# A transformer step's state-space mixer: its tiles re-ordered, conditioning loads in 1 MB steps, outputs of four tiles together

## The reference, cut to what matters

```python
ada = silu(c) @ ada_w + ada_b                      # 1024 x 6144: sh_m, sc_m, gt_m, sh_f, sc_f, gt_f
h = rms_norm(x, mix_pre_g) * (1 + sc_m) + sh_m
u, q, k, v, g_s, g_a = split(h @ w_in)             # u: 512 wide
bu = einsum('gpc,bsgc->bsgp', b_bar, u)            # 32 groups x 64 states, complex
state[t] = lam_bar * state[t-1] + bu[t]            # along 256 tokens
y = gelu(einsum('gcp,bsgp->bsgc', c_mat, state).real + d * u)
y = y * sigmoid(y @ w_glu)
q, k = rope(q), rope(k); y_a = attention(q, k, v)
merged = sigmoid(g_s) * (y @ w_s) + sigmoid(g_a) * (y_a @ w_a)
```

## Time and profile before

| | us |
|---|---|
| median of 3 runs | 2422.41 (2419.97 to 2429.88) |
| the profiled execution, its own time | 2422.49 |
| its span on the core | 2420.4 |
| PE busy | 2221.8 (92% of the span) |
| DVE busy | 960.2 (40%) |
| ACT busy | 605.2 (25%) |
| POOL busy | 27.4 (1%) |
| DMA, mean | 262 GB/s |

### The profile page before, as it was taken

One profiled execution on the slowest core, in us unless ns is written; L12 is line 12 of the kernel. 1 busy time (PEld: TensorE's weight loads), 2 busy tenths in 40 slices (PEclk: granted clock), 3 DMA queues, 4 the chain that ended last, 5 costly groups with the idle time before them and its releaser, 6 DMA issues.

```text
span 2420.4 us, 26402 instructions
## 1 busy us (share of the span) xinstructions
PE 2221.8 (92%) x10794; PEld 1292.1 (53%) x10794; DVE 960.2 (40%) x1683; ACT 605.2 (25%) x991; POOL 27.4 (1%) x44
## 2 busy tenths in 40 slices
PE   5888987999999899989975999989999999999998
PEld 3336842333333333333321888556887887555887
DVE  6782132222222222221213555344555554363655
ACT  2103020110101001001101443344434443154443
POOL 0010000000000000000000000000000000100000
PEclk9999989999999999999987999989999999999999
DMA  7534239999999999999997344224543453412541
GB/s 312 205 143 187 109 119 428 427 423 428 428 427 422 427 428 420 427 428 427 420 428 333 149 164 184 111 88 157 209 165 160 196 208 113 157 66 105 194 171 79
DMA packets 40765, 633.64 MB, mean 262 GB/s; under 512 B 4800, under 2 KB 4800, under 8 KB 5728
## 3 DMA queue, kind: packets, MB, share of 16 engines
q1 hardware_dynamic: 40640, 631.90, 63.4%
HBM read 630.84 MB, written 1.05 MB: 261 GB/s over the span
## 4 chain that ended last, share of the span: by engine, by line
PE 68%; DMA 18%; DVE 3%; ACT 2%; issue 1%; SPq 0%; ACTq 0%; DVEq 0%
DMA piece<-in_moe 18%; PE bank L1768 10%; PE bank L1684 10%; PE bank L1686 9%; PE bank L1685 9%; PE bank L599 6%; PE bank L1803 5%; PE bank L1218 3%; PE bank L1181 2%; PE bank L1749 2%; PE bank L1827 2%; PE bank L1013 1%; PE bank L1185 1%; PE bank L2088 1%; PE bank L1022 1%
## 5 line engine op out<-in xcount | busy, mean ns | idle before, releaser
L1768 PE MATMUL bank<-piece,xeT 128*64 128x512 f32 (+1 forms) x2304 | 453.1, 630 | 73.9 <-DMA piece<-in_moe 70.9
L1690 DVE TENSOR_TENSOR ffn_lo<-slot,ffn_hi 128x2048 fp32r<-128x2048 f32 x132 | 302.1, 2292 | 170.7 <-ACT ffn_hi L2213 165.1
L1768 PEld LDWEIGHTS bank<-piece,xeT 128*64 128x64 f32 (+1 forms) x2304 | 136.3, 133 | 357.9 <-issue 331.7
L1684 PE MATMUL bank<-ffn_hi,hT_hi 128*128 128x512 f32 x704 | 280.6, 399 | 8.4 <-DVE hT_lo L523 6.0
L2213 ACT ACTIVATE ffn_hi<-slot 128x2048 fp32r<-128x2048 f32 x132 | 251.7, 1913 | 130.2 <-PE bank L1686 115.2
L1686 PE MATMUL bank<-ffn_hi,hT_lo 128*128 128x512 f32 x704 | 275.5, 391 | 0.0
L1685 PE MATMUL bank<-ffn_lo,hT_hi 128*128 128x512 f32 x704 | 274.8, 390 | 0.0
L1875 DVE TENSOR_TENSOR hT<-hT,bank 128x512 f32<-128x512 f32 x144 | 92.2, 683 | 271.1 <-PE bank L1827 264.8
L599 PE MATMUL bank<-slot,hT 128*128 128x512 f32 (+1 forms) x384 | 169.2, 590 | 0.0
L1922 DVE TENSOR_SCALAR work<-bank 128x256 f32<-128x256 f32 x60 | 25.5, 425 | 355.2 <-PE bank L1775 355.2
L1684 PEld LDWEIGHTS bank<-ffn_hi,hT_hi 128*128 128x128 f32 x704 | 132.7, 189 | 38.1 <-issue 8.5
(11 more groups left out here) (610 smaller groups left out, 2336.9 us busy)
## 6 DMA issues: line engine op xcount, KB each, us to landing
piece<-in_moe SPq DMA_DIRECT2D x192, 2048.0 KB, 25.4
slot<-in_ffn SPq DMA_DIRECT2D x44, 3072.0 KB, 10.4
slot<-in_ada SPq DMA_DIRECT2D x6, 3072.0 KB, 10.0
slot<-in_merge SPq DMA_DIRECT2D x4, 3072.0 KB, 13.7
slot<-in_nsa_in SPq DMA_DIRECT2D x5, 2048.0 KB, 7.5
slot<-in_w_in SPq DMA_DIRECT2D x4, 2048.0 KB, 9.0
slot<-in_ada SPq DMA_DIRECT2D x3, 2560.0 KB, 9.0
slot<-in_hy_in SPq DMA_DIRECT2D x3, 2048.0 KB, 7.7
```

What stands on the lines that cost most here:

```text
L1684: pe.matmul(out, left[0], right[0], start=start, stop=False)
L1690: return dve.tensor_tensor(lo, x, hi.bitcast(F32), ALU.subtract)
L1768: pe.matmul(bank[n * c:n * (c + 1), :], x[:, kt, :], w[i][:, at:at + 512], start=kt == 0, stop=False)
```

## The change

1. **Outputs of four tiles together.** `outputs(q)` does the 16 matmuls of four tiles in one portion, the four tiles' matmuls interleaved, so that neighbours write to different 32-partition strips of the bank. It stands after the projections of tiles 4, 8, 12 and after the last tile. R gets six buffers: two in `ssm_r`, two each in the unused last 1 MB of ring slots 1 and 2; DVE waits for outputs only from tile 6 on, and for whole groups.
2. **Conditioning in 1 MB steps.** The six portions become 16 steps of four matmuls, one per tile, each on a load of its own of 1 MB in one of three thirds of slot 0; the bias and gain rows come as loads of 0.5 MB ("tails"). A step's load waits for the step three before it.
3. **Projection weights in halves.** q, k, v weights come as six loads of 1 MB in two halves of slot 2; PE does three projection matmuls per tile from tile 0 on, and none ahead of tile 0. At each half's end a drain of PE signals `qkv_half`.
4. **Angles earlier.** Sets 0 and 1 are made before `ada_vector(0)`, set 2 before the u copy, set 3 after tile 2; tile 0 needs three sets (`trig_done` 6).
5. **Rotary turn.** POOL's half goes to DVE. Both halves stand at the stage's end, behind the last skip, `ada_vector(2)` and the last v read.
6. `ada_vector(2)` moves from before tile 13 to behind the last skip, so the last four broadcasts wait for it.
7. The names of six semaphores are merged into two (`rows_dve`, `rows_pool`), with the counts that belong to that; nothing else in the other blocks changes.

```diff
+    def part(name, src, lo, width, slot, sub, done):
+        count[slot, sub] += 16
+        plan[name] = Part(src, lo, width, slot, 2048 * sub, held[slot, sub], sems[slot, sub], count[slot, sub])
+        order.append(plan[name])
+        held[slot, sub] = done
...
+    def qkv(h):
+        part(f"qkv{h}", ("w_in", 1 + h // 2), 2048 * (h % 2), 2048, 2, h % 2, (sig["qkv_half"], h + 1))
...
+        part(f"step{i}", ("ada", 3 * (g + 1) + n), ADA_GROUP * ADA_PARTS[n].index(kt), ADA_GROUP, 0, (i + g) % 3, (sig["ada_ready"], 3 + i + 1))
...
+    for what in ("q0 q1 s0 s1 s2 s3 s4 s5 q2 s6 s7 t1 q3 s8 s9 q4 s10 s11 s12 s13 q5 s14 s15 t2").split():
+        {"q": qkv, "s": ada_step, "t": ada_tail}[what[0]](int(what[1:]))
```

```diff
@@ ssm_vector
-        if j == 0:
-            dve.wait_ge(s["trig_done"], 8)
+        if jj == 0:
+            dve.wait_ge(s["trig_done"], 6 if q == 0 else 8)
...
-        if j >= 2:
-            dve.wait_ge(s["ssm_y_ready"], j - 1)
-        R = k["ssm_r"][:, j % 2, :, :, :]
+        if j >= SSM_ROWS:
+            dve.wait_ge(s["ssm_y_ready"], (j - SSM_ROWS) // SSM_Q + 1)
+        R = ssm_rows(k, j)
@@ ssm_tensor
-        pe.wait_ge(s["rotated"], j + 1)
...
+        pe.wait_ge(s["rotated"], SSM_Q * (q + 1))
         for n_, (c, trig, part) in enumerate(((0, 0, 0), (1, 1, 1), (2, 0, 1), (2, 1, 0))):
-            mm = pe.matmul(out, k["c_mix"][:, c, 32 * j:32 * j + 32], R[:, trig, part, :], start=n_ == 0, stop=n_ == 3)
+            for jj in range(SSM_Q):
+                j = SSM_Q * q + jj
+                mm = pe.matmul(k["ps"][6 + q % 2][32 * jj:32 * jj + 32, 0:S], k["c_mix"][:, c, 32 * j:32 * j + 32], ssm_rows(k, j)[:, trig, part, :], start=n_ == 0, stop=n_ == 3)
...
+        if at % KT == KT - 1:
+            pe.drain().then_inc(s["qkv_half"], 1)
...
+        for m in range(3 * j, 3 * j + 3):
+            project(m)
+        if j >= SSM_Q and j % SSM_Q == 0:
+            outputs(j // SSM_Q - 1)
+        if 10 <= j < 14:
+            ada_wide_tensor(k, pe, j - 10)
+        ada_step_tensor(k, pe, j)
+    outputs(SSM_TILES // SSM_Q - 1)
@@ the block of DVE
+            ssm_angles(f, dve, 1)
             ada_vector(f, dve, 0)
...
+            ssm_vector(f, dve, range(0, 3))
             ssm_angles(f, dve, 3)
+            ssm_vector(f, dve, range(3, 6))
             project_read(f, dve, 1, 2, qkv_dst, (0,), (2, 3))
+            ssm_vector(f, dve, range(6, 9))
             ada_vector(f, dve, 1)
+            ssm_vector(f, dve, range(9, 11))
             project_read(f, dve, 1, 2, qkv_dst, (1,), (2, 3))
+            ssm_vector(f, dve, range(11, 16))
+            ssm_skip(f, dve, 3)
             ada_vector(f, dve, 2)
             project_read(f, dve, 1, 2, qkv_dst, (2,), (2, 3))
+            for t in range(TT):
+                dve.wait_ge(*((s["proj_act"], 3) if t == 0 else (s["proj_dve"], 3)))
...
```

More of the change, by code:

```diff
@@ L63 @@
 SSM_Q = 4
+SSM_ROWS = 6
 HEADS, HD = 8, 64
@@ L161, in __init__ @@
         self.src, self.width, self.slot, self.free, self.landed = src, width, slot, free, landed
+class Part:
+    def __init__(self, src, lo, width, slot, at, free, sem, landed):
+        self.src, self.lo, self.width, self.slot, self.at, self.free, self.sem, self.landed = src, lo, width, slot, at, free, sem, landed
 class Batch:
@@ L304, in ada_tensor, with ada_step_tensor @@
     mm.then_inc(s["ada_ready"], 1)
+def ada_step_tensor(k, pe, i):
+    s = k["sig"]
+    g, kt = divmod(i, KT)
+    it = k["plan"][f"step{i}"]
+    bank = k["ps"][g]
+    pe.wait_ge(it.sem, it.landed)
+    for c in range(4):
+        at = it.at + c * 512
+        mm = pe.matmul(bank[32 * c:32 * c + 32, :], k["cond"][:, KT + kt:KT + kt + 1].to_broadcast([P, 32]), k["ring"][it.slot][:, at:at + 512], start=kt == 0, stop=kt == KT - 1)
+    mm.then_inc(s["ada_ready"], 1)
 def ada_vector(k, dve, g):
     s, vs = k["sig"], k["vs"]
-    it = k["plan"][f"ada{3 * g + 2}"]
+    if g == 0:
+        it, at = k["plan"]["ada2"], 2 * ADA_GROUP
+    else:
+        it = k["plan"][f"tail{g}"]
+        at = it.at
+        dve.wait_ge(it.sem, it.landed)
     r, bank = k["ada_r"][:, g, :], k["ps"][(4, 0, 1)[g]]
-    bias, gain = (k["ring"][it.slot][:, 2 * ADA_GROUP + i * 512:2 * ADA_GROUP + (i + 1) * 512] for i in range(2))
-    dve.wait_ge(s["ada_ready"], 3 * g + 3)
+    bias, gain = (k["ring"][it.slot][:, at + i * 512:at + (i + 1) * 512] for i in range(2))
+    dve.wait_ge(s["ada_ready"], 3 + KT * g)
     vs.mark(dve.tensor_tensor(r, bank, bias, ALU.add))
@@ L782, in angles_of @@
 def angles_of(k, q):
[L784 removed]
+    if q == 1:
+        scratch = k["rows"][:, 0:2 * D]
+    elif q == 3:
+        scratch = k["ring"][2][:, 4096:6144]
+    else:
+        scratch = k["ssm_r"][:, :, :, :, :].rearrange("p a b c d -> p (a b c d)")
+    scratch = scratch.rearrange("p (a b d) -> p a b d", a=2, b=SSM_Q)
     return scratch[:, 0, :, :], scratch[:, 1, :, :]
@@ L855, in inputs, with outputs, project @@
         mm.then_inc(s["bu_ready"], 1)
-    def outputs(j):
-        q, jj = divmod(j, SSM_Q)
-        if jj == 0 and q >= 2:
+    def outputs(q):
+        if q >= 2:
             pe.wait_ge(s["gelu_in"], q - 1)
-        if j == 0:
+        if q == 0:
             pe.wait_ge(s["gcol_done"], 1)
             pe.wait_ge(s["ssm_prep_dve"], 2)
-        pe.wait_ge(s["rotated"], j + 1)
-        out = k["ps"][6 + q % 2][32 * jj:32 * jj + 32, 0:S]
-        R = k["ssm_r"][:, j % 2, :, :, :]
+        pe.wait_ge(s["rotated"], SSM_Q * (q + 1))
         for n_, (c, trig, part) in enumerate(((0, 0, 0), (1, 1, 1), (2, 0, 1), (2, 1, 0))):
-            mm = pe.matmul(out, k["c_mix"][:, c, 32 * j:32 * j + 32], R[:, trig, part, :], start=n_ == 0, stop=n_ == 3)
+            for jj in range(SSM_Q):
+                j = SSM_Q * q + jj
+                mm = pe.matmul(k["ps"][6 + q % 2][32 * jj:32 * jj + 32, 0:S], k["c_mix"][:, c, 32 * j:32 * j + 32], ssm_rows(k, j)[:, trig, part, :], start=n_ == 0, stop=n_ == 3)
         mm.then_inc(s["ssm_y_ready"], 1)
-    def project(lo, hi):
-        project_tensor(k, pe, ["w_qkv0", "w_qkv1", "w_qkv2"], 2, [512] * 3, k["hT"], KT, 2, range(lo, min(hi, 6 * KT)), (2, 3))
+    def project(m):
+        j, at = divmod(m, 2 * KT)
+        half, t, kt = at // KT, at // 4 % 2, at // KT * 4 + at % 4
+        it = k["plan"][f"qkv{2 * j + half}"]
+        u = 2 + 2 * j + t
+        if at % KT == 0:
+            pe.wait_ge(it.sem, it.landed)
+        if kt == 0 and j >= 1:
+            pe.wait_ge(s["proj_act"] if t == 0 else s["proj_dve"], j + 1)
+        lo = it.at + (kt % 4) * 512
+        mm = pe.matmul(k["ps"][2 + u % 2][:, :], k["hT"][:, kt, t * P:(t + 1) * P], k["ring"][it.slot][:, lo:lo + 512], start=kt == 0, stop=kt == KT - 1)
+        if kt == KT - 1:
+            mm.then_inc(s["proj_ready"], 1)
+        if at % KT == KT - 1:
+            pe.drain().then_inc(s["qkv_half"], 1)
     inputs(0)
-    project(0, 2 * KT)
     for j in range(SSM_TILES):
@@ L3170, in _ @@
             project_read(f, act, 0, 2, qkv_dst, (1,), (2, 3))
-            ada_wide_scalar(f, act, 0)
             gelu_scalar(f, act, 1)
-            for i in range(1, 4):
+            for i in range(4):
                 ada_wide_scalar(f, act, i)
```

113 lines of the change are left out of this document (50 added, 63 removed).

## The result

| | before | changed |
|---|---|---|
| median, same chip, 4 runs each | 2424.34 us (2419.97 to 2429.88) | 2390.93 us (2387.75 to 2394.07) |
| ratio, 95% interval | | 0.9864 (0.984 to 0.9888) |
| the profiled execution, its own time | 2422.49 us | 2394.07 us |
| its span | 2420.4 us | 2392.2 us |
| turn of q and k on PE (L941, now L1007) | 197.32 us | 167.42 us |

The account below looks back on a forecast made before the run. PE and DVE, waiting for each other, bound the state stage. DVE's 148.1 plus 0.1 and 1.9 gave 150.1; tail 15.2 and 1.5 gave 166.8 instead of 197.32, 30.5 us off 2422.5: 2392.0 us, range 2386 to 2405.

Parts of the forecast that it names:

- What bounds: State stage, 126.2 us: PE and DVE wait for each other; a us won here is a us at the end.
- Outputs, 1.9 us a portion: PE in the state stage: interleaved matmuls run four at a time, so four portions cost 7.6 us instead of 29.4.
- the rival worked out from that rule: Output portions: weight loads do not overlap, 5.6 us per portion, a gain of 18 us, 2404 us; chance 0.08.
- DVE's sum, 148.1: DVE in the state stage: 89.2 us of work from 58.9, so tile 15's rotated rows are complete at 148.1.
- PE's sum, 147.2: PE without the last outputs: 85.0 us from 57.66, plus a 4.5 us gap during angle set 3, done at 147.2.
- the row of 3.40 us: Profile before: an outputs portion took 3.40 us instead of 1.84 after a 2.94 us wait; hence 1.5 added to the broadcasts.
- Angles: DVE: tile 0 starts at 58.9 instead of 74.0; set 1 fills a 7.12 us wait, delaying at most 0.1.
- That cost disappears: DVE beside POOL's rotary turn: a tile's two scans took 3.28 us instead of 1.27; without that turn this goes.
- Loads: SP's queue: a 1 MB load lands in 4.8 us, is issued 9.6 us ahead of use, and is hidden.
- What the rival feared: SP's queue: loads become a chain behind other entries, 38 us slower, 2461 us; chance 0.03.
- The tail: From the last outputs to the turn of q and k: 15.2 us, plus 1.5 for slow broadcasts, ending at 166.8.
- From there on all as before, 30 us earlier.: After the turn of q and k: everything runs as in the kernel before, only 30 us earlier.

Follow-up runs that it names:

- run 1: The changed kernel with each portion's output matmuls issued tile after tile instead of interleaved; 2403.93 us, ratio 0.9897 to 0.9952.
- run 7: run 4 with the three reads of token half 1 of q, k and v moved from DVE to ACT; 2387.07 us, ratio 0.9835 to 0.9883.
- Run 2: The changed kernel with the angle sets back in their old places and tile 0 waiting for all of them; 2399.69 us, ratio 0.9867 to 0.9925.
- run 3: The changed kernel with one half of the rotary turn given back to POOL, beside tiles 8 and 9; 2394.99 us, ratio 0.9853 to 0.9907.
- run 6: The changed kernel with conditioning in its six old portions and loads of 2.5 or 3 MB, `ada_vector(1)` behind tile 6; 2409.72 us, ratio 0.9926 to 0.9968.
- Run 4: The changed kernel with `ada_vector(2)` ahead of the last skip instead of behind it; 2385.66 us, ratio 0.9825 to 0.9875.
- run 5: The kernel before with only the interleaved four-tile outputs and six buffers of rotated rows; 2413.12 us, ratio 0.9961.
- run 8: run 7 with seven projection matmuls at tile 3, loads reordered, one DVE drain less per four tiles; 2388.6 us, ratio 0.984 to 0.9876.

## Why the prediction was right, point by point

- **What bounds.** The claim was that the stage is on the path and a microsecond there is one at the end. The mark moved by 29.9 us (predicted 30.5), the span by 28.2. It holds but for the 3.1 us below.
- **Outputs, 1.9 us a portion.** Measured 1.76 to 1.93. Here the rule that the prediction set against the rows fails. The Trainium skill ("TensorE: Matmul & The Clock Gate", on packing small matmuls) has weight loads overlap only where the row group differs. All 128 rows are in use in each of these matmuls, and 16 of them, each with its own weights, still pass in 1.86 us; the rival worked out from that rule said 5.6. Even the order that run 1 chose stays at 4.5, below it.
- **DVE's sum, 148.1.** Measured 148.5. The three drains of 0.28 us were missing from it; the rest came out 0.4 lower.
- **PE's sum, 147.2.** Measured 148.9, and this is the step that was off. Three terms were too small. The six drains were taken at 0.1 us each, with no row behind it; from start to start they cost 0.15 to 0.50, 2.1 together in place of 0.6. The price of a slow clock behind a wait was charged to the broadcasts, from the row of 3.40 us, but not to the inputs and projections behind the 4.5 us gap, where it was 1.6. And a step of conditioning took 0.99 us in place of 0.95, 0.6 in all. The inputs, at 0.97 us from start to start in place of 1.06, gave 1.6 of it back, and the first three portions, at 1.75 to 1.87, another 0.3. So PE and not DVE was last, by 0.4 where the prediction had DVE last by 0.9; run 7 shows it, since 1.2 us less on DVE left the last outputs where they were. The two sums lay so close that the total hardly suffered, 150.8 for 150.1.
- **Angles.** Tile 0 at 58.91, predicted 58.9; set 1 delayed the first conditioning rows by 0.15 us, predicted 0.1 at most; the gap of 4.61 us, predicted 4.5. Run 2 puts the price of undoing it at 7.5 to 7.9 us.
- **POOL's turn.** "That cost disappears": run 3 puts it at 5.8 us at the end of the last outputs and at 4.1 to 4.7 at the turn of q and k.
- **Loads.** No wait for a step. What the rival feared, a load held up by another entry in front of it, is what run 6 shows in part: waits of 8.9 and 9.0 us, with 3.3 and 7.9 us between a free slot and the issue. The prediction was right that three rotating thirds, in this order of SP's list, hide the loads, and never said how much of the gain hangs on them; run 6 puts size and order together at 14.6 us.
- **The tail.** 15.2 + 1.5 predicted from the end of the last outputs, 16.6 measured. The broadcasts took 5.55 us for the predicted 3.8 + 1.5. The rotary turns ended at 162.0 with 3.9 us to spare (predicted 161.4 and 2.5).
- **"From there on all as before, 30 us earlier."** This failed. The stretch to the first experts took 152.50 us in place of 149.40 at a granted clock of 0.95 in place of 0.97, with no instruction changed, and 152.49 in the second run of the changed kernel. Run 4 gives 149.94 by taking the wait ahead of the broadcasts away. It doesn't show in the total, because the medians of this comparison lie 33.4 us apart and the profiled spans only 28.2; the interval of the ratio allows 27 to 39 us. That the predicted time met the median to 1.1 us is therefore partly luck, while the mark at the turn of q and k, met to 0.6, is not touched by it.
- **The parts don't add up.** Undone one at a time, the parts (with the order of SP's list in the last) move the mark by 10.6, 7.5, 4.7 and 14.6 us, 37.4 together, against 29.9 for all. Done alone on the kernel before, the outputs bring 8.3. Each part takes its gain from waits that another part could also have opened or closed; that is argued from the waits in runs 5, 6 and 8 and would explain why the prediction's two sums, of PE and of DVE, came out right where a sum of single gains would not.

Of the versions measured, run 4 is the best to keep: one pair of lines exchanged, 2385.66 us, ratio 0.985. Run 7 is as fast and changes more. Not tried: run 6 with its loads in another order, run 8 with the idle time before the last outputs closed as well, and a way to start the stage's second half without any wait of PE.

## What to carry to other kernels

Where two engines feed each other, add up each engine's own work between two fixed points and go by the later sum; the price of a single edit says little before both are known, and after the edit the engine with the smaller sum will wait. Matmuls with 32 columns of weights should be issued so that neighbours lie in different column strips: here 16 of them cost as much as four had. When the order of an engine's last steps is free, put first what another engine waits for: exchanging two calls on DVE gave 5 us here, half of it behind the place that was changed. And where one queue issues all loads, see for each what stands in front of it: in run 6 a free slot stood empty for 3.3 and 7.9 us behind a load that was still waiting for another place.
